# Three edits in one transformer kernel: gate rows in two row groups, a first softplus by chunks, two mixer outputs copied unscaled

## The reference, cut to what matters

```
# layer 0: mLSTM, 4 heads. ig, lf: input gate and log forget gate, one row of 512 per head
b     = cumsum(lf)
log_d = where(causal, b[t] - b[s] + ig[s], -inf);  m_t = max(log_d over s)
d     = exp(log_d - m_t)
h_out = num / maximum(abs(den), exp(-m_t))
# layer 1: stick-breaking attention, 16 heads of 64
z     = q @ k.T * scale
a     = exp(log_sigmoid(z) + suffix sums of log_sigmoid(-z));  out = a @ v
# layer 2 (16 meta tokens in front, 528 columns): the mixer
u     = rmsnorm(h);  proj = u @ w_in          # 36 blocks of 128 outputs
q, f_logit, i, g, v_pool, gates = split(proj) # f: the forget gate of a chunked recurrence (hgrn)
```

## Time and profile before

| | |
|---|---|
| time, median of 3 runs | 2469.6 us (2469.06, 2469.6, 2475.74) |
| the profiled execution's own time | 2464.64 us |
| its span in the profile | 2463.3 us |
| mean granted TensorE clock | 0.989 |
| PE busy | 2378.0 us, 97% |
| DVE, ACT, POOL busy | 1004.6 us, 877.7 us, 1070.3 us |
| DMA queue of the weights, share of 16 engines | 24.2% |

### The profile page before, as it was taken

The page is one execution under the profiler, slowest core; times in us unless marked ns, Lnnn a source line. Parts: engine busy times, 40 slices in busy tenths (PEclk is TensorE's granted clock), DMA queues, the critical chain, the costliest instruction groups (busy, mean ns, idle before and its releaser), DMA issues.

```text
span 2463.3 us, 31077 instructions
## 1 busy us (share of the span) xinstructions
PE 2378.0 (97%) x12860; PEld 2002.6 (81%) x12860; DVE 1004.6 (41%) x1529; ACT 877.7 (36%) x1275; POOL 1070.3 (43%) x811
## 2 busy tenths in 40 slices
PE   7999999999999999999999999998899999999997
PEld 6766877788888887778778888888888998899886
DVE  3236813622210623757236222105573445745403
ACT  4324523522222424755235222224344233322321
POOL 6422753344455442037433444553344443544452
PEclk9999999999999999999999999999999999999999
DMA  4211431222232221014212222222111222222232
GB/s 157 86 60 52 137 103 52 78 94 94 94 103 103 87 95 59 1 62 144 86 52 86 94 95 95 101 103 90 65 35 62 94 87 84 88 95 94 94 103 69
DMA packets 64012, 211.40 MB, mean 86 GB/s; under 512 B 8832, under 2 KB 13056, under 8 KB 63872
## 3 DMA queue, kind: packets, MB, share of 16 engines
q1 hardware_dynamic: 59120, 206.00, 24.2%
q10 hardware_dynamic: 4752, 3.42, 0.5%
HBM read 207.29 MB, written 2.10 MB: 85 GB/s over the span
## 4 chain that ended last, share of the span: by engine, by line
PE 84%; DVE 10%; ACT 3%; issue 2%; DMA 1%; ACTq 0%; POOL 0%; SPq 0%; DVEq 0%
PE ps L412 68%; PE ps L518 5%; DVE u_lo L1500 2%; PE ps L740 1%; DVE x L1521 1%; DVE ps L1519 1%; PE ps L756 1%; PE ps L835 1%; PE ps L761 1%; PE ps L676 1%; PE ps L784 1%; DMA w_land<-in_units 1%; PE ps L656 1%; PE ps L869 1%; DVE acc L1592 0%
## 5 line engine op out<-in xcount | busy, mean ns | idle before, releaser
L2150 POOL TENSOR_TENSOR w_lo<-w_land,w_hi 128x512 fp32r<-128x512 f32 x768 | 1025.3, 1361 | 1303.4 <-ACT w_hi L965 1303.4
L412 PE MATMUL ps<-u_hi,w_hi 128*128 128x512 f32 (+3 forms) x2560 | 824.2, 348 | 32.9 <-DVE u_lo L1500 13.8
L412 PE MATMUL ps<-u_lo,w_hi 128*128 128x512 f32 (+3 forms) x2560 | 817.1, 346 | 0.0
L412 PE MATMUL ps<-u_hi,w_lo 128*128 128x512 f32 (+3 forms) x2560 | 813.8, 344 | 0.0
L412 PEld LDWEIGHTS ps<-u_hi,w_hi 128*128 128x128 f32 x2560 | 457.5, 189 | 109.5 <-DVE u_lo L1500 20.2
L965 ACT ACTIVATE w_hi<-w_land 128x1024 fp32r<-128x1024 f32 x384 | 401.0, 1050 | 331.1 <-DMA w_land<-in_units 323.8
L412 PEld LDWEIGHTS ps<-u_lo,w_hi 128*128 128x128 f32 x2560 | 455.1, 189 | 62.0 <-issue 1.4
L412 PEld LDWEIGHTS ps<-u_hi,w_lo 128*128 128x128 f32 x2560 | 455.9, 189 | 60.3
L412 PE MATMUL ps<-hid_hi,w_hi 128*128 128x512 f32 (+1 forms) x594 | 220.2, 371 | 0.0
L412 PE MATMUL ps<-hid_lo,w_hi 128*128 128x512 f32 (+1 forms) x594 | 219.7, 370 | 0.0
L412 PE MATMUL ps<-hid_hi,w_lo 128*128 128x512 f32 (+1 forms) x594 | 219.4, 369 | 0.0
(11 more groups left out here) (306 smaller groups left out, 2794.3 us busy)
## 6 DMA issues: line engine op xcount, KB each, us to landing
w_land<-in_units SPq DMA_DIRECT2D x384, 512.0 KB, 3.2
x<-in_xT SPq DMA_DIRECT2D x4, 528.0 KB, 7.4
arena<-in_memT ACTq DMA_DIRECT2D x2, 1024.0 KB, 5.1
outT<-x SPq DMA_DIRECT2D x16, 128.0 KB, 1.7
arena<-in_masks ACTq DMA_DIRECT2D x1, 448.0 KB, 3.2
arena<-in_consts ACTq DMA_DIRECT2D x1, 296.0 KB, 3.7
consts<-in_consts SPq DMA_DIRECT2D x1, 256.0 KB, 8.1
arena<-in_consts ACTq DMA_DIRECT2D x1, 256.0 KB
```

The costliest lines, as they stand in the source:

```text
L412: ins = pe.matmul(ps[:, bank, at:at + c1 - c0], w, rhs(k, c0, c1)[which], start=first and h == 0, stop=last and h == 2)
L2150: pool.tensor_tensor(w_lo[:, u % LAND, half], w_land[:, u % LAND, half], w_hi[:, u % RING, half].bitcast(F32), ALU.subtract).then_inc(*uni ...
```

## The change

Three edits at three places, independent of each other.

**Gate rows.** exp(-m) is now written to partitions 32 to 35 (`floor_rows`), and the selection matrix has a second copy of its rows there, so that the two matmuls of a head read different groups of 32 partitions. The four pairs no longer stand in one place: the `uT` transposes and head 0's pair come after unit 5, head 1's after the first half of unit 6, head 2's after its second half, head 3's after the first half of unit 7. DVE takes `uT` out first and computes `arguments(h)` right after head `h`'s copy, ACT `decays(h - 2)` after head `h`'s square, with one unit's rounding ahead of the last.

**First softplus.** For head 1 of the first pair alone, ACT finishes a part (absolute, exponential, log1p) before it begins the other, DVE takes value 1 after lower 0, and PE waits for lower 1 ahead of all of block 0's sums.

**Two outputs unscaled.** ACT copies outputs 0 and 1 out of PSUM without `rstd`, in four copies between its squares 3 to 6; DVE multiplies them by `rstd` in place later. PE makes outputs 2 and 3 ahead of `norm_mean(6)`.

```diff
-    put("sel", np.arange(ML_H * P)[None, :] // P == s)
+    put("sel", (np.arange(ML_H * P)[None, :] // P == s) | (np.arange(ML_H * P)[None, :] // P == s - 32))
...
+        floor_rows = rows[32:36, 3, 0:S]
...
+                def broadcast(h):
+                    if h == 0:
+                        pe.wait_ge(*ml_gate_v.at(7))
+                        await_empty([2])
+                        for b in range(4):
+                            ins = pe.transpose(ps[:, 2, 4 * b:4 * b + 4], rows[0:4, 0, b * P:(b + 1) * P], ident[0:4, 0:4])
...
+                    b = 2 * (h % 2)
+                    for bank, sel, row in ((b, sel_all[0:4, cols], w1), (b + 1, sel_all[32:36, cols], floor_rows)):
...
+                        pe.matmul(ps[:, bank, :], sel, row, start=True, stop=True).then_inc(*full[bank].up())
...
-                by_token("ml_v", u_tok, 4, [(5, broadcasts)])
+                by_token("ml_v", u_tok, 4, [((5 + (h + 1) // 2, (h + 1) % 2), lambda h=h: broadcast(h)) for h in range(ML_H)])
...  # sums
+                        if b == 0 and at == 1:
+                            pe.wait_ge(*sb_lo_at.at(2 * at + 2))
...  # mix, PE
-                output("mix_in", 2, PAIRS[:20], u_rhs, TWO, six(2))
+                outputs("mix_in", PAIRS[:20], u_rhs, TWO, six, 2, 4)
                 norm_mean(6)
-                outputs("mix_in", PAIRS[:20], u_rhs, TWO, six, 3, FIRST_FILLER)
+                outputs("mix_in", PAIRS[:20], u_rhs, TWO, six, 4, FIRST_FILLER)
...  # out_and_norm, ACT, among the squares
+                    if n == 6 and 3 <= k < 7:
+                        unscaled((k - 3) // 2, (k - 3) % 2)
+            def unscaled(o, part):
+                act.wait_ge(*ready_at["mix_in", o])
+                (c0, c1), b = TWO[part], banks_at["mix_in", o][part]
+                ins = act.activation(mix_dst(o)[:, c0:c1], ps[:, b, 0:c1 - c0], ACT.Copy)
...  # mLSTM, ACT
-                        act.activation(w2, w2, ACT.Exp, scale=-1.0).then_inc(*ml_gate_s.up())
+                        act.activation(floor_rows, w2, ACT.Exp, scale=-1.0).then_inc(*ml_gate_s.up())
...
-                        decays(0)
-                        decays(1)
+                            if h:
+                                hi_to(UNIT["ml_v"] + LEAD + 7 + (h == 3))
+                            if h >= 2:
+                                decays(h - 2)
...  # stick-breaking, ACT, i == 0
+                        for n in range(2):
+                            absolute(1, i, n)
+                            exponential(1, i, n)
+                            log1p(1, i, n)
...  # mLSTM, DVE
+                            if h < 2:
+                                dve.wait_ge(*emptied_at["ml_bc", h, 0])
+                                arguments(h)
...  # softplus, DVE
-                    value(1)
-                    own()
-                    lower(0)
+                    if i or not h:
+                        value(1)
+                        own()
+                        lower(0)
+                    else:
+                        own()
+                        lower(0)
+                        value(1)
...  # mix, DVE
+                    if o < 2:
+                        dve.wait_ge(*emptied_at["mix_in", o])
+                        dve.tensor_tensor(mix_dst(o)[:, :], mix_dst(o)[:, :], rstd[:, :], ALU.mult)
```

More of the change, by code:

```diff
@@ L519, in by_token @@
                                                     start=k == 0 and n == 0, stop=k == DT - 1 and n == 2)
-                        ins.then_inc(*unit_done.up())
-                        if 4 * g + j in between:
-                            between[4 * g + j]()
+                            if kk:
+                                ins.then_inc(*unit_done.up())
+                            if (4 * g + j, kk) in between:
+                                between[4 * g + j, kk]()
                     for b in range(n_blocks):
@@ L550, in mlstm @@
                 outputs("ml_og", SQUARE, u_rhs, ONE, four)
[L552 to L567, removed]
-                by_token("ml_v", u_tok, 4, [(5, broadcasts)])
+                def broadcast(h):
[4 more added lines that the diff above has]
+                            ins = pe.transpose(ps[:, 2, 4 * b:4 * b + 4], rows[0:4, 0, b * P:(b + 1) * P], ident[0:4, 0:4])
+                        ins.then_inc(*full[2].up())
+                        holds("ml_uT", [2], full[2].now())
+                    cols = slice(h * P, (h + 1) * P)
+                    b = 2 * (h % 2)
+                    for bank, sel, row in ((b, sel_all[0:4, cols], w1), (b + 1, sel_all[32:36, cols], floor_rows)):
+                        if h == 0 and bank == 1:
+                            pe.wait_ge(*ml_gate_s.at(7))
+                        await_empty([bank])
+                        pe.matmul(ps[:, bank, :], sel, row, start=True, stop=True).then_inc(*full[bank].up())
+                        holds(("ml_bc", h, bank % 2), [bank], full[bank].now())
+                by_token("ml_v", u_tok, 4, [((5 + (h + 1) // 2, (h + 1) % 2), lambda h=h: broadcast(h)) for h in range(ML_H)])
                 def scores(h):
@@ L792, in first_scores @@
                     z(0, 0)
-                by_token("sb_v", u_tok, 4, [(3, first_scores)], lambda g, b: 4 - g + b)
+                by_token("sb_v", u_tok, 4, [((3, 1), first_scores)], lambda g, b: 4 - g + b)
                 sums(0, 0)
@@ L1040, in out_and_norm @@
                     square_step(n, k)
+                    if n == 6 and 3 <= k < 7:
[4 more added lines that the diff above has]
+                ins = act.activation(mix_dst(o)[:, c0:c1], ps[:, b, 0:c1 - c0], ACT.Copy)
+                if part:
+                    ins.then_inc(*emptied_by["mix_in", o])
             def norm_end(n, name):
@@ L1336, in stick_breaking @@
                             weights(0, i, n)
-                    for n in range(2):
-                        absolute(1, i, n)
-                    if i:
+                        for n in range(2):
[3 more added lines that the diff above has]
+                    else:
+                        for n in range(2):
+                            absolute(1, i, n)
                         weights(0, i, 0)
-                    exponential(1, i, 0)
-                    if i:
+                        exponential(1, i, 0)
                         weights(0, i, 1)
-                    exponential(1, i, 1)
-                    for n in range(2):
-                        log1p(1, i, n)
+                        exponential(1, i, 1)
+                        for n in range(2):
+                            log1p(1, i, n)
                     if i + 1 < SB_H // 2:
```

16 lines of the change are left out of this document (7 added, 9 removed).

## The result

The changed kernel takes 2455.9 us, median of 7 runs (2451.5 to 2461.3). The kernel before, in 7 runs beside it, took 2469.1 (2465.2 to 2475.7). The forecast was 2456. The profiled execution is 2455.89 us, its span 2454.6, where before's were 2464.64 and 2463.3.

The account below looks back on a forecast made before the run. PE, busy 97% of the span, was taken as the bound. Gains of 5.6 (gate rows), 2.6 (softplus) and 5.3 us (unscaled outputs), 13.5 in all, took 2469.6 to 2456.1, given as 2456 us; range 2449 to 2462.

Parts of the forecast that it names:

- both waits in full: First softplus: new waits of 0.2 us at block 0 and 0 to 0.5 us for ACT's weights, taken at their largest.
- three steps of 0.43: Gate rows: a pair's four instructions take three steps, 1.3 us a pair, 5.2 us for four.
- rival (b): Gate rows: the pairs run fully abreast, 0.86 us each; total gain 15.2 us, 2454 us; chance 0.08.
- The change of rows: Gate rows: going between 64 and 128 rows costs 0.3 us per visit, 1.2 us for four visits.
- (e): Gate rows: every visit keeps the clock at 0.50, the edit loses 12.0 us; total 2474 us; chance 0.05.
- (c): Clock still falls at the gate rows and gives nothing back at the softplus; gain 10.2 us, 2459 us; chance 0.13.
- the half of the 2.07 us: First softplus: of 2.07 us that the sums lose to the low clock, half comes back, 1.0 us.
- The stray wait for `lower` in block 0: First softplus: PE needs the second part at 969.9, it ends about 970.1; a new wait of 0.2 us.
- The wait for ACT's weights: First softplus: head 1's second `z` waits for weights queued behind ACT's passes, another 0 to 0.5 us.
- Rival (d): Mixer: the gap only moves, as DVE sets the recurrence's start; gain 8.2 to 10.8 us, 2459 to 2461 us; chance 0.10.
- the cover of about 6 us: Mixer: unit 6 is ready at 1711.0, PE wants it at 1717.2; each microsecond late beyond 6 would cost one.

Follow-up runs that it names:

- all_again: The changed kernel once more, no edit, on another chip: 2450.7 us, 0.9936 of the kernel before.
- one_group: Kernel before plus the gate-rows edit alone, four visits kept, but both rows of a head read from partitions 0 to 3: 2467.7 us, one run.
- padded_z: Changed kernel plus three unread matmuls between head 1's first `z` run and head 0's next: 2449.9 us, 0.9921 of the kernel before.
- gates_only: Kernel before plus the gate-rows edit alone: 2462.6 us, 0.9986 of the kernel before.
- softplus_only: Kernel before plus the first-softplus edit alone: 2466.0 us, 0.9997 of the kernel before.
- mixer_only: Kernel before plus the edit of two unscaled outputs alone: 2463.9 us, 0.9987 of the kernel before.
- softplus_again: Same code as softplus_only, the kernel before plus the first-softplus edit alone, run once more: 2463.1 us, one run, beside 2468.9 of the kernel before.
- padded_both: padded_z plus four more unread matmuls in the wait at the start of the recurrence: 2450.7 us, 0.9921 of the kernel before.

## Why the prediction was right, point by point

**The total.** 13.5 us foretold, 13.2 between the medians, 13.35 in the stages. That is closer than the terms are, and partly luck: edit 1 gave 1.3 more, edit 2 in the first profile 1.2 less, edit 3 0.3 less, and these cancel. The totals themselves are less sharp than the agreement looks, 8.7 us by the spans, 14.8 by the ratio, and 17.6 between the medians in all_again's group. Two bounds of the prediction do not come out of its own terms. With nothing from the clock and both waits in full, edit 2 is 1.8 - 0.2 - 0.5 = 1.1, not 1.3; and the bounds as given, with 5.3 for edit 3, add up to 10.5 to 16.3, where 9 to 17 was taken. Neither touches the outcome.

**Edit 1, 5.6 against 6.9: right mechanism, a term mis-sized.** The place before was 12.2 us as worked out (23.22 less v's 48 x 0.23). Now it is 16.30 - 11.04 = 5.3, not 6.6. The mis-sized term is the pair: three steps of 0.43, 1.3 us, because a2 and b2 were thought to stand in line. They run fully abreast, 0.86, so four pairs cost 3.4 and not 5.2; rival (b) held in this step. The prediction's own row pointed there: in the earlier trace rows 4.3 us of work took 2.30, where fully abreast would be 2.15. Its three steps rested on the order of a1, a2, b1, b2, but the first two instructions start at 147.08 and 147.20, so b1 does not wait for a2. The change of rows, put at 0.3 a visit, is 0.4: 1.06 - 0.86 = 0.2 inside a visit, and 2.98 - 12 x 0.23 = 0.2 in the group behind it. The transposes are 0.28 (0.2). 3.4 + 1.6 + 0.3 = 5.3. The clock stayed at 1.00, so (e) and the half of (c) that is about this edit fell; one_group shows that this half was near, for with longer visits the clock did fall after the first.

TensorEngine Tiling (Array Packing) of the Trainium skill, Key Properties, lets different tiles multiply in parallel and drains the engine at a change of mode. The trace agrees with both halves: 0.86 us for a pair (0.85 less than in one group), and 0.2 us on each side of a visit.

**Edit 2, 2.6 against 1.4, or 2.3.** The earlier start was 1.8 foretold and 1.81 measured. The start of the sums is 1.81 us nearer in all four profiles with the edit alone or with the others (7.14 to 7.15 us after the first `z`, 8.95 to 8.96 in the seven without). The term that failed in the first profile is the half of the 2.07 us that was to come back: the clock fell inside `z`, the low stretch moved with the sums instead of shrinking, and they took 5.13 us where they took 4.76 before (4.83 in the prediction, by the chain's 975.07). For this profile the second half of rival (c) was right. In the three other profiles with the edit the clock held through `z` and through a wait of 0.99 us, as near to the forecast's 1 us as can be, and fell in the sums, which took 4.33 to 4.53. On average the sums take 4.6 with the edit and 5.1 without, so that the clock gives 0.5 us back and not 1.0. Over the profiles at hand B is 11.77 with the edit (12.28, 11.64, 11.48, 11.68) and 14.09 without (seven from 13.71 to 14.37), 2.3 us less, so the first pair was at the poor end: 1.8 + 0.5 where 1.8 + 1.0 - 0.2 was foretold. The stray wait for `lower` in block 0, put at 0.2, does not show as a row. The wait for ACT's weights (0 to 0.5) is 0.29 where the clock holds, and nothing where the sums are slow. That it is a matter of clock and not of waits, padded_z shows: with it at 1.00, B is 10.77.

**Edit 3, 5.3 against 5.0.** PE goes from output 2 to output 11 without a wait. 59.77 us from 1684.17 to 1743.94 less 0.89 for the ones is 58.9, where 58.7 was taken; the ones are 0.89, not 0.73. These two make the 0.3. Rival (d) fell: the wait for DVE ahead of the recurrence is 4.1 us before and after. ACT's copies delayed nothing that PE waits for; `rstd` was there 1.3 us after the ones (1.8 foretold), and the cover of about 6 us was not needed.

**What stays open.** The totals of the single edits make 0.9970 and the whole 0.9940 and 0.9936, while their stages add up. The mean granted clocks show where the difference lies. They are 0.9867 over the 29 runs of the kernel before, 0.9870, 0.9859 and 0.9861 for gates_only, softplus_only and mixer_only, but 0.9890 for the changed kernel and 0.9903 in all_again, with 0.9852 for the kernel before beside it. Within each kernel's own runs the time falls by some 1.6 us for 0.001 more of clock, by a straight line through them. An estimate with that slope takes all of them to one clock: there the single edits lie 3.4, 1.3 and 4.3 us below the kernel before, 9.0 together, and the whole change 8.7 (8.0 in all_again). So at one clock the totals add up too, and the rest of the whole's gain goes with a higher granted clock, part of it that of the stages A and B themselves. Why the kernels with one edit were not granted more is not shown. Nor is it settled what makes the clock fall or hold in the recurrence, or why softplus_only stayed at half clock for 20 us in one profile. Its second profile, softplus_again, whose sums start at 967.04, is low in them and back at full clock by 971:

```profile
962.00:971.00 9.00, 8.01 (x37) 6.58 (x37) 5.75 (x9) 8.49 (x13) 0.00 (x0) 0.81 0.00 0
971.00:981.00 10.00, 10.00 (x57) 7.50 (x58) 6.02 (x10) 6.78 (x11) 0.00 (x0) 1.00 0.00 0
```

The fastest version is padded_z or padded_both, 0.9921 of the kernel before; between them and the changed kernel lie 0.15% to 0.2% by ratios to the kernel before, within the intervals, so that only the stage B, 10.77 in both, shows the step.

## What to carry over

Small matmuls that stand one behind the other and read few partitions can be put in different groups of 32 rows, in pairs: here that halved them, and once it was done the place where they stand was worth far less (6.35 us against 0.57). Where an output waits only for a factor per row, take it out unscaled and multiply later, so that its banks come free. And compare changes of a few microseconds by the stages that they touch, not by one span: here an untouched stage differed by 5 us between two executions of one kernel.

## What was unexpected of the hardware

- Two fp32 matmuls of 4 x 128 by 4 x 512 in different row groups run fully abreast: a visit with one pair takes 1.06 us against 1.91 in one group, sixteen instructions 3.87 us against 6.9 one behind the other. The second product's first instruction does not wait for the first product's second. A change between 4 and 128 rows costs 0.2 us in each direction.
- A busy PE need not keep its clock: in the changed kernel's first profile, from 958 to 965, in `z` and the sums, it was busy 6.75 of 7 us and was granted 0.50 to 0.53. Three unread matmuls over the full array between two runs of 64-row matmuls, 0.79 us, went with 1.00 through `z` and the sums in both profiles that had them; all eleven without lost clock in these sums.
- Once low, it may stay low through some 20 us in which PE is hardly idle (19.97 of 20 us busy in softplus_only, at 0.54 and 0.50), and the same code in another execution is back at 1.00 some 4 us after its sums began. In the recurrence of the changed kernel the clock makes 5 us between two executions, as much as the third edit is worth.
